# Triangular inversion from all four quarters of TensorE in a hybrid decoder layer

## The reference

```
h = h + concat([nsa(p), rwkv7(p)]) @ w_out      # p = rms_norm(h) @ w_in
h = h + cross_attention(h, mem)                 # 4 heads of 256, 256 memory tokens
h = h + moe(rms_norm(h))                        # top 4 of 32 experts

# rwkv7: a scan over 256 steps in 8 heads of 64
state = state * w_t + (state @ a_t) b_t + v_t k_t
y_t   = state @ r_t
# nsa: 8 heads in 2 groups; compressed keys (15 of them), selected and window keys
o = g0 * o_cmp + g1 * o_slc + g2 * o_win
```

## Time and profile before

| | |
|---|---|
| Median of 3 runs | 1292.21 us |
| The profiled execution | 1294.45 us, its span 1292.7 us |
| PE, DVE, ACT, POOL busy | 1241.8, 360.0, 191.8, 54.9 us |
| DMA | 442.61 MB, mean 342 GB/s |
| Mixed stage (from tok 0 to w_out) | 105.1 to 265.6 us |
| w_out, cross-attention, router | 265.6 to 387.3 us |
| Experts | 387.3 us to the end |

### The profile page before, as it was taken

One profiled execution on the slowest core, in us unless ns is written; L12 is line 12 of the kernel. 1 busy time (PEld: TensorE's weight loads), 2 busy tenths in 40 slices (PEclk: granted clock), 3 DMA queues, 4 the chain that ended last, 5 costly groups with the idle time before them and its releaser, 6 DMA issues.

```text
span 1292.7 us, 19115 instructions
## 1 busy us (share of the span) xinstructions
PE 1241.8 (96%) x7750; PEld 634.2 (49%) x7750; DVE 360.0 (28%) x846; ACT 191.8 (15%) x436; POOL 54.9 (4%) x104
## 2 busy tenths in 40 slices
PE   9999899899999999999999999999999998989897
PEld 8888788688883433323233333434333232333332
DVE  4466653432226212212121221212212121212111
ACT  3332354412320000000000000000000000000001
POOL 6210001101010000000000000000000000000000
PEclk9999899899999999999999999999999999999999
DMA  7342411068179999999999999999999999999997
GB/s 266 126 152 103 164 36 66 3 275 375 59 316 371 428 426 427 428 430 429 427 427 427 426 395 421 427 428 428 428 429 428 428 429 428 429 427 428 430 427 295
DMA packets 36055, 442.61 MB, mean 342 GB/s; under 512 B 4000, under 2 KB 4128, under 8 KB 6304
## 3 DMA queue, kind: packets, MB, share of 16 engines
q1 hardware_dynamic: 35424, 440.76, 81.7%
q10 hardware_dynamic: 576, 1.05, 0.2%
HBM read 440.75 MB, written 1.05 MB: 342 GB/s over the span
## 4 chain that ended last, share of the span: by engine, by line
PE 65%; DMA 31%; DVE 2%; ACT 1%; issue 1%; POOL 0%; SPq 0%; DVEq 0%; ACTq 0%; POOLq 0%
DMA sb_ring<-in_mlp_w 31%; PE ps L965 22%; PE ps L992 9%; PE ps L323 9%; PE ps L923 3%; PE ps L933 2%; PE ps L677 2%; PE ps L821 2%; PE ps L772 2%; PE ps L543 2%; PE ps L945 1%; PE ps L336 1%; PE ps L980 1%; PE ps L418 1%; PE ps L401 1%
## 5 line engine op out<-in xcount | busy, mean ns | idle before, releaser
L965 PE MATMUL ps<-sb_ring,sb_xv 128*64 128x512 f32 x1960 | 439.7, 596 | 29.4 <-DMA sb_ring<-in_mlp_w 28.5
L965 PEld LDWEIGHTS ps<-sb_ring,sb_xv 128*64 128x64 f32 x1960 | 133.5, 137 | 311.5 <-issue 252.7
L992 PE MATMUL ps<-sb_ring,sb_xv 128*64 128x512 f32 x1024 | 228.5, 596 | 1.3 <-DMA sb_ring<-in_mlp_w 1.3
L1558 DVE TENSOR_SCALAR sb_early<-ps 128x256 f32<-128x256 f32 x64 | 27.2, 424 | 646.5 <-PE ps L965 646.5
L992 PEld LDWEIGHTS ps<-sb_ring,sb_xv 128*64 128x64 f32 x1024 | 71.7, 137 | 134.6 <-issue 132.8
L1598 ACT ACTIVATE sb_early<-sb_early 128x256 f32<-128x256 f32 (+2 forms) x69 | 28.2, 408 | 510.1 <-DVE sb_early L1558 507.3
L1598 ACT ACTIVATE sb_early<-ps 128x512 f32<-128x512 f32 (+4 forms) x46 | 23.6, 515 | 280.2 <-PE ps L992 265.9
L933 PE MATMUL ps<-sb_early 64*128 64x512 f32 x248 | 61.6, 615 | 0.0
L923 PE MATMUL ps<-sb_early,sb_hnT 128*128 128x128 f32 x512 | 59.9, 275 | 0.0
L923 PEld LDWEIGHTS ps<-sb_early,sb_hnT 128*128 128x128 f32 x512 | 58.4, 192 | 0.2 <-DVE sb_early L1439 0.2
L323 PE MATMUL ps<-sb_hnT,sb_wsl 128*128 128x256 f32 x256 | 56.1, 379 | 0.0
(11 more groups left out here) (359 smaller groups left out, 1068.3 us busy)
## 6 DMA issues: line engine op xcount, KB each, us to landing
sb_ring<-in_mlp_w SPq DMA_DIRECT2D x184, 2048.0 KB, 20.7
sb_wsl<-in_w_front SPq DMA_DIRECT2D x31, 1024.0 KB, 4.8
sb_ring<-in_mlp_w SPq DMA_DIRECT2D x4, 1024.0 KB, 17.9
sb_wsl<-in_mlp_w SPq DMA_DIRECT2D x3, 1024.0 KB, 7.6
sb_spare<-in_mlp_w SPq DMA_DIRECT2D x2, 1024.0 KB, 9.1
sb_wsl<-in_w_values SPq DMA_DIRECT2D x1, 1120.0 KB, 5.0
sb_wsl<-in_w_front ACTq DMA_DIRECT2D x4, 256.0 KB, 6.4
sb_ox<-in_mem_T SPq DMA_DIRECT2D x1, 1024.0 KB, 10.8
```

Source lines behind the costliest of these rows:

```text
L965: mm = pe.matmul(psum[64 * half:64 * half + 64, 4 + n, :], xgT[:, k, SLOTS * par:SLOTS * par + SLOTS], w[:, at + 512 * half:at + 512 * hal ...
L992: mm = pe.matmul(psum[64 * o2:64 * o2 + 64, 7, :], actT[:, 2 * n + m, 64 * q:64 * q + 64], ring[:, at + 512 * o2:at + 512 * o2 + 512], sta ...
L1558: dve.tensor_scalar(gl, psum[:, 4 + n, 0:256], 7.0, None, ALU.min).then_inc(sem("glu"), 1)
```

## The change

The inversion is rewritten. Products change halves: an operand from the upper partitions can write to lower ones and the other way round, each of the two row halves into its own bank. P is no longer accumulated by DVE; instead the factors I + D2, I + D4, I + D8 are made (DVE adds the identity) and multiplied: 15 steps, of which ACT copies 11, DVE copies two and adds the identity to them, and only adds the identity in two. The new buffers B5 to B7 lie in `spare`, so item parts (4, 0) and (4, 1) are loaded later. Compressed probabilities are transposed for 4 heads at once (`turnc`, padded to 32 columns each) and the compressed values lie in a padded 128-row buffer. `xv` comes in 8 halves. The squares of `xk` are added by POOL before one product. The lora products of decay and rate alternate. `xpv` works on whole heads with 256 columns. `ORDER` and `CROSS` are new lists.

```diff
-        INV = [("D2", "copy", "DT", "D", "B1"), ("D2T", "copy", "D", "DT", "B2"),
-               ("D4", "copy", "B2", "B1", "B3"), ("D4T", "copy", "B1", "B2", "B4"),
-               ("P2", "add", "B2", "PP", "PP"), ("D8T", "copy", "B3", "B4", "B1"),
-               ("P4", "add", "B4", "PP", "PP"), ("P8", "add", "B1", "PP", "PP"),
-               ("P8T", "turn", "PP", None, "B2"), ("T1", "copy", "E1T", "PP", "B3"),
-               ("M1", "add", "B2", "B3", "PP"), ("M1T", "turn", "PP", None, "B2"),
-               ("T2", "copy", "E2T", "PP", "B3"), ("M2", "add", "B2", "B3", "PP")]
+        INV = [("D2", "DT", "D", "B2", None), ("D2T", "D", "DT", "B3", "PP"), ("F1", "DT", None, None, "B5"),
+               ("D4", "B3", "B2", "B6", None), ("D4T", "B2", "B3", "B7", "B1"), ("Q1", "PP", "B5", "B4", None),
+               ("F8T", "B6", "B7", None, "B2"), ("Q2", "B1", "B4", "B3", None), ("P8", "B2", "B3", "PP", None),
+               ("P8T", "PP", None, "B5", None), ("T1", "E1T", "PP", None, "B6"), ("M1", "B5", "B6", "B7", None),
+               ("M1T", "B7", None, "B2", None), ("T2", "E2T", "B7", None, "B3"), ("M2", "B2", "B3", "PP", None)]
...
+        ORDER = [('xk', 0), ('score', 0), ('tok', 0), ('cmpin',), ('xkn', 0), ('xk', 1), ('score', 1), ('parts', 0),
+                 ('xkn', 1), ('xk', 2), ('parts', 1), ('g3',), ('xkn', 2), ('xk', 3), ('xkn', 3), ('inv', 0),
+                 ('inv', 1), ('xv', 0), ('inv', 2), ('cmp',), ('cmpout',), ('tok', 3), ('cmpsc',), ('inv', 3),
+                 ('turnc', 0), ('xv', 1), ('turnp', 0), ('turnp', 1), ('score', 2), ('akv',), ('inv', 4), ('inv', 5),
+                 ('pv', 0), ('score', 3), ('inv', 6), ('inv', 7), ('xv', 2), ('pv', 1), ('turnp', 2), ('score', 4),
+                 ('inv', 8), ('xv', 3), ('turnp', 3), ('pv', 2), ('inv', 9), ('inv', 10), ('score', 5), ('tok', 1),
+                 ('pv', 3), ('inv', 11), ('xv', 4), ('inv', 12), ('turnc', 1), ('turnp', 4), ('turnp', 5),
+                 ('inv', 13), ('pv', 4), ('score', 6), ('inv', 14), ('score', 7), ('tok', 2), ('pv', 5), ('qt',),
+                 ('z',), ('turnp', 6), ('turnp', 7), ('chunk', 0), ('pv', 6), ('chunk', 1), ('y', 0), ('pv', 7),
+                 ('chunk', 2), ('xv', 5), ('chunk', 3), ('ymean', 0), ('y', 1), ('yvar', 0), ('xv', 6), ('ymean', 1),
+                 ('xv', 7), ('yvar', 1)]
+        CROSS = [('project', 0), ('project', 1), ('norm', 0), ('score', 0), ('score', 1), ('norm', 1),
+                 ('project', 2), ('turn', 0), ('turn', 1), ('score', 2), ('score', 3), ('norm', 2), ('project', 3),
+                 ('score', 4), ('score', 5), ('pv', 0), ('turn', 2), ('turn', 3), ('turn', 4), ('norm', 3),
+                 ('score', 6), ('score', 7), ('pv', 1), ('turn', 5), ('turn', 6), ('turn', 7), ('pv', 2), ('pv', 3)]
...
             def inv_step(s):
-                name, kind, lhs, rhs, _ = INV[s]
-                for q in range(2):
...
-                    t = tile("inv", s, q, freed=(own, value))
-                    for n in range(8):
-                        m = 8 * q + n
-                        for c in range(2):
-                            r = slice(64 * c, 64 * c + 64)
-                            moving = identc[r, :] if kind == "turn" else BUF[rhs][r, m, :]
-                            mm = pe.matmul(t[r, n * CH:(n + 1) * CH], BUF[lhs][r, m, :], moving,
-                                           start=True, stop=True)
+                both = [tile("inv", s, h, freed=inv_done(name, h)) for h in range(2)]
+                for n in range(8):
+                    for h in range(2):
+                        r = slice(64 * h, 64 * h + 64)
+                        for o in range(2):
+                            moving = identc[r, :] if rhs is None else BUF[rhs][r, 8 * o + n, :]
+                            mm = pe.matmul(both[h][64 * o:64 * o + 64, n * CH:(n + 1) * CH],
+                                           BUF[lhs][r, 8 * o + n, :], moving, start=True, stop=True)
...
-                pe.matmul(t[:, 0:T], o256[:, :], xsq[:, 0, :], start=True, stop=False)
-                pe.matmul(t[:, 0:T], o256[:, :], xsq[:, 1, :], start=False, stop=True) \
-                  .then_inc(sem("tile_ready"), 1)
+                pe.matmul(t[:, 0:T], o256[:, :], xsq[:, 0, :], start=True, stop=True).then_inc(sem("tile_ready"), 1)
...
+            def turnc_step(tt):
+                pe.wait_ge(sem("cmp_probs"), tt + 1)
+                t = tile("pc", tt, freed=("ptc", tt + 1))
+                for g in range(NSA_G):
+                    mm = pe.transpose(t[:, g * P:(g + 1) * P],
+                                      sc_c[:, tt, 4 * g:4 * g + 4, :].rearrange("p a b -> p (a b)"), ident[:, :])
...
+            def xk_step(j):
+                pool.wait_ge(sem("kx_squared"), j + 1)
+                pool.tensor_tensor(xsq[:, 0, :], xsq[:, 0, :], xsq[:, 1, :], ALU.add).then_inc(sem("kx_squares"), 1)
...
+                elif n == 4:
+                    sp.wait_ge(sem("inv_copied"), 2 * len(COPIED))
+                    if half:
+                        sp.wait_ge(sem("pv_done"), 8)
...
-                if j == J_XV[1]:
+                if j == J_OUT[2]:
                     piece_ahead(4, 0)
-                    piece_ahead(4, 1)
...
             piece_ahead(0, 0)
             piece_ahead(0, 1)
+            piece_ahead(4, 1)
```

236 lines of the change are left out of this document (121 added, 115 removed).

## The result

The changed kernel takes 1283.75 us in the median of four runs (1283.42 to 1285.51), the one before 1292.91 (1291.49 to 1293.8). The ratio is 0.9935, 95% interval 0.9915 to 0.9955: 9.2 us less, where 18.2 had been forecast. It is 0.7% of the time; the interval leaves out no change. The range (1265 to 1284) holds it, by a quarter of a microsecond; the number of rival 2 (1282) is the nearest.

A forecast was written before the change was run, and what follows sets the result against it. Stage 4 was taken as bound by DMA bytes, stages 1 to 3 by PE's timeline. Savings 12.5 + 5.7 + 0 + 1 = 19.2 us, less 1 for switches, 18.2: 1292.2 to 1274.0 us, range 1265 to 1284.

The forecast's parts named there:

- rival 2: Gaps take the gain: shorter steps, unshortened copies, PE waits 1 us more at each level; 8 us less gain, 1282; chance 0.18.
- Bound and lever: Stage 4 lasts as long as its bytes take; each microsecond off stages 1 to 3 comes off the total.
- Inversion: Inversion steps in the mixed stage: 28.1 us become 15 steps of 1.04, 15.6 us; 12.5 us saved.
- bound of 58 ns: Slow bound per inversion product, taken from the state products: 15 steps would take 27.8 us, saving 0.3.
- rival 3: Neighbours on one row half hinder each other in the inversion: step 1.85 us, 0.3 saved instead of 12.5, 1286; chance 0.09.
- rule of the Trainium skill: Weight loads overlap running matmuls only if row groups differ; by it the inversion would go at 58 ns a product.
- Smaller products: Savings on xk norm 1.8, transposes 1.3, compressed values 0.5, lora 1.6 and cross-attention's values 0.5; 5.7 us in sum.
- one microsecond of the cross-attention: Gaps in the cross-attention: the wait before turn 0 goes, the last values wait longer; 1 us saved, between 0 and 3.
- 0.5 us of its values: Cross-attention's values: 8 products of 0.89 us become 16 of 0.41; 0.5 us saved.
- Stalls and clock: Mixed stage: 12.3 us of gaps and 4 of low clock, 16.3 against 16 before; net 0, bounds -7 and +7.
- low clock that was expected: Mixed stage at 1.2 GHz: 2.5 us around cmpout and 1.5 at the chunks, 4 us in all.
- I cost the chain at nothing: Inversion's 8 dependent levels, 21 us inside some 100, cost nothing beyond the counted stalls; copies hidden by idle ACT and DVE.

The follow-up runs named there:

- rows_alternate: Changed kernel with the inversion step's two inner loops exchanged, so that neighbouring products lie in different row halves; 1285.42 us, 0.9944 of the kernel before.
- inv_alone: Kernel before with only the new inversion, its steps in the old order with one more place, and two item parts loaded later; 1300.24 us, 1.0044.
- two_quarters: Changed kernel in which each inversion product writes only the quarter beside its own row half; 1292.2 us, 0.9997 of the kernel before.
- after_again: The changed kernel measured once more, unchanged, as yardstick for the others; 1285.76 us, 0.9939 of the kernel before.
- xkn3_later: Changed kernel with the last xk norm two inversion steps later in the list; 1284.57 us, 0.9926 of the kernel before.
- loads_apart: Changed kernel with the load of the last xv weights issued only when inversion step 7 is done; 1285.09 us, 0.9936 of the kernel before.
- spread2: Changed kernel with one xv half between tok 3 and the compressed scores and the next behind turnc 0; 1282.01 us, 0.9917 of the kernel before.

## Why the forecast was half right

- **Bound and lever: right.** Stage 4 stays bound by its bytes and starts 8.1 us earlier, where 18.2 were forecast. From there to the end it took 902.9 us after and 905.4 before, with the same work; the other kernels' traces lie between 902.7 and 906.1. So some 2 of the 10.6 us in the profiled pair are stage 4's own spread, which the forecast has at nothing, and it is luck that the time lies inside the range. (The slices are misread by one: counted from 0, as the prediction counts, 388 us lie in slice 12, with 371 GB/s, and slice 13 begins at 420. Nothing hangs on it.)
- **Inversion: right.** 1.09 us a step against 1.04; 15 steps at full clock are 16.4 where 28.1 were, 11.7 saved of 12.5. The bound of 58 ns and rival 3 are out: 34 ns a product, and `rows_alternate` has no faster step. g3, at 1.03 in the same trace, stays a little faster. By the rule of the Trainium skill weighed there (TensorE: Matmul & The Clock Gate, Part 3, packing small matmuls) the changed order would have been slower than that of `rows_alternate`; the traces disagree, 1.09 us against 1.09.
- **Smaller products: nearly.** In the mixed stage all work fell by 14.4 of 15.1. The lora saves 1.0 of 1.6 (44.21 to 47.97 for its 24 records, 4.72 before). The one microsecond of the cross-attention did not come: stage 3 lasts 121.6 against 121.8, with 3.6 us of gaps in both, and the 0.5 us of its values went with it.
- **"Stalls and clock", net 0: the step that failed.** It counted 12.3 of gaps and 4 of clock, 16.3 in all against 16 of before. Measured by the account: 15.5 and 8.4, 23.9 against 16.8, so 7.1 us worse. Of the 12.3 us of gaps that it names 10.1 are there: score 0 0.8, xkn 3 2.4, hidden layer 1.6, a bank 0.7, qt 2.0 and probabilities 0.5, chunk steps 2.1 for 1; xkn 0 and turnc 0 do not wait. 5.4 are there that it doesn't name, above all 2.69 without instructions and 2.14 ahead of step 12, each with a low clock behind it: 8.2 us for the two, more than the whole miss of this step. The low clock that was expected cost 2.5 us around cmpout; it lasted 10.2 us there and cost 5.1. At the chunks, where 1.5 were left for it, it is gone (1.00 from 220 on).
- **"I cost the chain at nothing": wrong at one place.** The reason given, half-idle ACT, says nothing on order: M1's copies stood behind an instruction that itself waited 4.12 us. That is rival 2's family, though not its mechanism: in the changed kernel no step waits a microsecond for its own copies alone (0.42 us is the longest). In the old order both are seen (`inv_alone`: 3.75 us behind exps, 1.36 for the copies alone).
- **Common cause.** 143.6 us of work had waits hidden in it, for copies and for instructions, that became visible at 129. `two_quarters` to `after_again` shows this with the list and the table equal (13.7 less of work, 6.2 more of gaps and clock), `inv_alone` shows it at its worst. Against the 18.2 us the experts start 10.1 too late: 7.8 in the mixed stage (7.1 of it this step), 1.0 ahead of it, 1.3 in stage 3.

Not settled: why a removed gap comes back at the clock in one kernel (`xkn3_later`, `loads_apart`: 11.4, 11.8) and not in another, and what moving the load of weights alone would do to the stop; in `spread2`, which has it down to 0.38, products, blocks and load all lie elsewhere.

## What to carry to other kernels

When products of PE get cheaper, count the saving as work and then go through the list again for waits that were covered: here about half of the saving came back as gaps and low clock. A copy on an in-order engine is as late as whatever waits ahead of it, so read what ACT stands still for, not how busy it is. Where a timeline names no releaser, look in the trace for a wait record of the sequencer that spans the gap: with one it is a wait, here once the longest gap of a kernel. Without one, count the records up to the gap, the sequencer's waits among them: if the counts of several kernels differ by multiples of 256, it is the supply of instructions. Then look at what the DMAs move just before, and keep loads of weights away from long runs of small products.

## What the runs showed of the hardware

Small products in close order can outrun their instructions: 25 stops of 0.15 to 3.94 us, all at places a multiple of 256 records apart, behind blocks that passed in 2.0 to 4.3 us; PE goes on 2.2 to 2.8 us after a packet of 16 KB starts, and that packet mostly comes when a running load of weights has ended. And four quarters of TensorE work at 34 ns a product of 64x64x64 whether neighbours share a row half or not, against 60 for two quarters.
